# Eight x0 projection panels spread over the forward-transform and spectral stages of a Hyena and gated-linear-attention kernel

## The reference, cut to what matters

```
z = short_conv(u @ w_in + b_in)            # (1024, 3072), three taps along the tokens
x0, x1, v = split(z, 3);  s = v * x1
g = filter(...)                            # taps, 2048 x 1024, divided by their absolute sums
y = irfft(rfft(s, 2048) * rfft(g, 2048))[:1024]
out = ((y + s * skip) * x0) @ w_out + b_out
```

## Time and profile before

| | |
|---|---|
| median of three runs | 2641.41 us |
| the profiled execution | 2642.06 us |
| its span on the core | 2640.3 us |
| TensorE busy | 2469.5 us (94%) |
| GpSimd, VectorE, ScalarE busy | 705.7, 1168.0, 653.2 us |
| mean granted TensorE clock | 0.97 |

### The profile page before, as it was taken

The page is one execution under the profiler, slowest core; times in us unless marked ns, Lnnn a source line. Parts: engine busy times, 40 slices in busy tenths (PEclk is TensorE's granted clock), DMA queues, the critical chain, the costliest instruction groups (busy, mean ns, idle before and its releaser), DMA issues.

```text
span 2640.3 us, 29602 instructions
## 1 busy us (share of the span) xinstructions
PE 2469.5 (94%) x11356; PEld 1979.7 (75%) x11356; DVE 1168.0 (44%) x1221; ACT 653.2 (25%) x800; POOL 705.7 (27%) x394
## 2 busy tenths in 40 slices
PE   7987997677999999999999789999999999999996
PEld 5765664443788888888888679898888787778885
DVE  7899564342623311331235693626262322430443
ACT  4102344344321100000012362626363101111011
POOL 2233112231233333333333312222212232233331
PEclk9998998898999999999999899999999999999998
DMA  4232216776111111111111120202021421211231
GB/s 190 74 126 87 81 63 218 154 172 141 32 43 46 49 51 51 48 48 48 64 48 56 48 96 25 72 24 71 27 69 48 185 91 59 64 40 60 91 120 71
DMA packets 61180, 208.11 MB, mean 79 GB/s; under 512 B 6198, under 2 KB 7928, under 8 KB 60986
## 3 DMA queue, kind: packets, MB, share of 16 engines
q1 hardware_dynamic: 46170, 161.05, 19.2%
q10 hardware_dynamic: 14944, 46.14, 5.9%
HBM read 162.08 MB, written 36.70 MB: 75 GB/s over the span
## 4 chain that ended last, share of the span: by engine, by line
PE 70%; DVE 3%; ACT 1%; issue 0%; ACTq 0%; DVEq 0%
PE ps L1071 59%; PE ps L476 4%; DVE T L1707 1%; PE ps L1315 1%; PE ps L523 1%; PE ps L542 1%; PE ps L505 1%; PE ps L544 1%; PE ps L543 1%; PE ps L1093 0%; DVE XN L1737 0%; PE ps L1102 0%; PE ps L447 0%; DVE X L2017 0%; DVE H L1730 0%; DVE T L1737 0%
## 5 line engine op out<-in xcount | busy, mean ns | idle before, releaser
L1071 PE MATMUL ps<-H,whi 128*128 128x512 f32 x4000 | 1088.3, 394 | 35.2 <-POOL wlo L1027 14.9
L1071 PEld LDWEIGHTS ps<-H,whi 128*128 128x128 f32 x4000 | 753.0, 189 | 208.2 <-issue 23.7
L1025 POOL CAST whi<-wraw 128x1024 fp32r<-128x1024 f32 x190 | 202.9, 1068 | 1808.7 <-issue 744.9
L1071 PE MATMUL ps<-H,wlo 128*128 128x512 f32 x2000 | 618.8, 391 | 0.0
L1027 POOL TENSOR_TENSOR wlo<-wraw,whi 128x1024 fp32r<-128x1024 f32 x194 | 490.8, 2530 | 58.3 <-ACT whi L610 43.1
L1071 PEld LDWEIGHTS ps<-H,wlo 128*128 128x128 f32 x2000 | 377.3, 189 | 79.6
L1071 PE MATMUL ps<-A,whi 128*128 128x512 f32 x1472 | 395.7, 391 | 6.4 <-DVE A L2049 4.9
L1071 PEld LDWEIGHTS ps<-A,whi 128*128 128x128 f32 x1472 | 277.0, 188 | 65.3 <-issue 5.3
L1071 PE MATMUL ps<-A,wlo 128*128 128x512 f32 x736 | 227.2, 390 | 0.0
L1071 PEld LDWEIGHTS ps<-A,wlo 128*128 128x128 f32 x736 | 138.7, 188 | 29.0
L1966 DVE TENSOR_TENSOR T<-ps,T 128x1024 f32<-128x1024 f32 x22 | 26.9, 1224 | 202.6 <-PE ps L1071 202.6
(11 more groups left out here) (342 smaller groups left out, 2587.9 us busy)
## 6 DMA issues: line engine op xcount, KB each, us to landing
wraw<-in_panels SPq DMA_DIRECT2D x181, 512.0 KB, 3.5
mw<-in_modp SPq DMA_DIRECT2D x24, 512.0 KB, 3.5
g<-gsp ACTq DMA_DIRECT2D x16, 512.0 KB, 2.6
wraw<-g SPq DMA_DIRECT2D x16, 512.0 KB, 10.9
s<-sa SPq DMA_DIRECT2D x16, 512.0 KB, 2.6
bs<-s SPq DMA_DIRECT2D x16, 512.0 KB, 6.9
YB<-yi ACTq DMA_DIRECT2D x32, 256.0 KB
kf<-in_kfft SPq DMA_DIRECT2D x16, 320.0 KB, 7.6
```

The costliest lines, as they stand in the source:

```text
L1025: nc.gpsimd.tensor_copy(whi[:, s, :, :], wraw[:, s, :, :]).then_inc(hi_made, 1)
L1071: last = mm(p[:, c * step:(c + 1) * step], w[:, ws, k, :], operand(act, a, k, c * step, step), start=(q == 0 and w is whi and a == 0), sto ...
```

## The change

1. **taps** replaces mix. It has the 16 tap rows alone, unrolled. TensorE makes values two rows ahead and then spreads (`tap_values(m+2)`, `tap_spread(m)`). ScalarE makes the absolute values (into ca or cb) and takes out odd rows, VectorE takes out even rows, SyncE stores both.
2. **sfwd** follows a list. It has four x0 panels among the pairs, and the tap norm moves to its front. `sn`, `st`, `sa` lie elsewhere, so that H stays whole, and there are four `sa` buffers.
3. **spec** has the other four panels, behind groups 1, 4, 7 and 10, in the PSUM tensor `ps[3]`. The spectral work has six banks: four for filter spectra, made one half ahead, one for the signal's spectrum and one for the inverse. VectorE multiplies in place into ga and gb, and `bl`, `kl` are made ahead of the products in its order. The result goes by whole rows to DRAM (`y1`, three `yi` buffers). SyncE reads it back in two halves of 2 MB for partitions 0 to 63 behind groups 13 and 14, and at the end in four pieces of 1 MB for partitions 64 to 127.
4. **inv** has 16 jobs of 256 columns, a piece of 256 channels after the other, with the tiles between.

The lists that set the order of inv, of sfwd and of the late panels:

```diff
-INV = [("rows", 0, 512, n2) for n2 in range(0, N2, 2)]
+INV = [("rows", 0, 256, 4 * _m) for _m in range(4)]
...
+SFWD = [("panel", 0), ("norm",), ("turn", 0), ("turn", 1)]
+for _i in range(PAIRS):
+    SFWD += [("dft", _i, 0), ("dft", _i, 1)]
+    if _i in (2, 5, 7):
+        SFWD.append(("panel", (2, 5, 7).index(_i) + 1))
+    if _i + 2 < PAIRS:
+        SFWD.append(("turn", _i + 2))
+X0_AFTER = (1, 4, 7, 10)
```

SyncE at the end of spec, with `EARLY` = 8:

```diff
+            def y_back(lo, hi, c0, w, k):
+                sp.dma_start(YB[lo:hi, :, c0:c0 + w], y1[lo:hi, :, c0:c0 + w]).then_inc(x_in[k], 16)
...
+                    y_back(0, 8 * EARLY, 512 * (g - 13), 512, g - 13)
+            for n in range(2 * GROUPS - 3, 2 * GROUPS):
+                sp.wait_ge(y1_out[n % 3], y1_stored(n))
+            for k in range(4):
+                y_back(8 * EARLY, P, 256 * k, 256, k)
```

TensorE, spec:

```diff
-                if n >= 2:
-                    pe.wait_ge(spec_ev, n - 1)
+                if n:
+                    pe.wait_ge(spec_ev, n)
...
             filter_spectra(0)
-            filter_spectra(1)
             for n in range(2 * GROUPS):
                 g, c = n // 2, n % 2
-                if n >= 2:
-                    filter_spectra(n)
+                if c and g in X0_AFTER:
...
+                    panel_mm(ps[3], e % 2, H, T, 8).then_inc(panel_done, 1)
+                if n + 1 < 2 * GROUPS:
+                    filter_spectra(n + 1)
                 pe.wait_ge(spec_lo, rows_made(n))
-
-                three(bank(c, 0), g, 0, bh[c][:, :], bl[c][:, :]).then_inc(spec_xm, 1)
+                if n:
+                    pe.wait_ge(spec_y, 2 * n)
+
+                three(bank(4), g, 0, bh[c][:, :], bl[c][:, :], None if c else panel_done).then_inc(spec_xm, 1)
                 if n:
                     inverse(n - 1)
```

ScalarE, taps:

```diff
+            for m in range(N2):
+                if m + 2 < N2:
+                    decay_rows(m + 2)
+                tap_abs(m)
+                if m % 2:
+                    o = spread_job(m)
+                    act.wait_ge(aux_done, A0["taps"] + o + 1)
...
+                    A_(gsp[1][:, :], ps[slot("taps", o)][:, :], ACT.Copy).then_inc(evac[slot("taps", o)], 1)
+                if m + 2 < N2:
+                    decays(m + 2)
```

ScalarE, spec:

```diff
+                if n:
+                    spec_inverse(n - 1)
+                if n + 1 < 2 * GROUPS:
+                    spectra_out(n + 1)
```

VectorE, spec:

```diff
             for n in range(2 * GROUPS):
-                c = n % 2
-                dve.wait_ge(spec_xm, n + 1)
...
+                g, c = n // 2, n % 2
                 if n + 1 < 2 * GROUPS:
                     rows_lo(n + 1)
-                if c == 0 and n // 2 + 1 < GROUPS:
-                    mats_lo(n // 2 + 1)
+                if c == 0 and g + 1 < GROUPS:
+                    mats_lo(g + 1)
...
+                dve.wait_ge(spec_xm, n + 1)
+                for q, t in enumerate((ga, gb)):
+                    dve.wait_ge(spec_g, 2 * n + q + 1)
+                    V_.tensor_tensor(t[c][:, :], ps[2][:, 0:512], t[c][:, :], ALU.mult).then_inc(spec_y, 1)
```

More of the change, by code:

```diff
@@ L959, in _ @@
             panels(N0["up2"] + 2, N0["lrx"])
[L960 removed]
+            sp.wait_ge(aux_done, A0["taps"] + 2 * N2)
             sp.dma_start(wup_h[:, :], d["wup"][:, 0:DK]).then_inc(wup_in, 16)
@@ new lines, in tap_values, with tap_spread @@
+            def tap_values(m):
+                o = tap_job(m)
+                free("taps", o)
+                pe.wait_ge(hbs_made, m + 1)
+                for c in range(2):
+                    last = mm(ps[slot("taps", o)][:, c * 512:(c + 1) * 512], hbs[m % 2][:, :],
+                              wtap[:, c * 512:(c + 1) * 512], start=True, stop=True)
+                last.then_inc(aux_done, 1)
+            def tap_spread(m):
+                o = spread_job(m)
+                free("taps", o)
+                pe.wait_ge(evac[slot("taps", tap_job(m))], turn("taps", tap_job(m)) + 1)
+                for c in range(2):
+                    last = mm(ps[slot("taps", o)][:, c * 512:(c + 1) * 512], cc("dft_g"),
+                              tap[m % 2][:, c * 512:(c + 1) * 512], start=True, stop=True)
+                last.then_inc(aux_done, 1)
@@ L1183, in forward @@
                             last.then_inc(aux_done, 1)
-            pe.wait_ge(const_in, 32)
-            turned(0)
-            for i in range(PAIRS):
-                if i + 1 < PAIRS:
-                    turned(i + 1)
-                forward(i)
-            free("tapnorm", 0)
-            pe.wait_ge(tap_sum, N2)
-            for e in range(KT):
-                last = mm(ps[slot("tapnorm", 0)][:, e:e + 1], gacc[:, e * P:(e + 1) * P], ones[:, 0:1],
-                          start=True, stop=True)
@@ L1196, in _, with tap_norm @@
-            last.then_inc(aux_done, 1)
-            for u in range(3 * PAIRS - 3, 3 * PAIRS):
+            def tap_norm():
+                o = sfwd_job("norm")
+                free("sfwd", o)
+                pe.wait_ge(tap_sum, N2)
+                for e in range(KT):
+                    last = mm(ps[slot("sfwd", o)][:, e:e + 1], gacc[:, e * P:(e + 1) * P], ones[:, 0:1],
+                              start=True, stop=True)
+                last.then_inc(aux_done, 1)
+            pe.wait_ge(const_in, 32)
@@ new lines, in _ @@
+            for kind, *j in SFWD:
+                if kind == "panel":
+                    n = N0["sfwd"] + j[0]
+                    o = sfwd_job("panel", j[0])
+                    pe.wait_ge(split_made, n + 1)
+                    free("sfwd", o)
+                    panel_mm(ps[slot("sfwd", o)], n % 2, H, T, 8).then_inc(panel_done, 1)
+                elif kind == "norm":
+                    tap_norm()
+                elif kind == "turn":
+                    turned(j[0])
+                elif j[1] == 0:
+                    forward(j[0])
@@ new lines, in _, with x0_conv @@
+            for m in range(N2):
+                tap_made(m)
+                if m and m % 2:
+                    o = spread_job(m - 1)
+                    dve.wait_ge(aux_done, A0["taps"] + o + 1)
+                    if m > 2:
+                        dve.wait_ge(g1_out[0], 16 * (m // 2))
+                    V_.tensor_copy(gsp[0][:, :], ps[slot("taps", o)][:, :]).then_inc(evac[slot("taps", o)], 1)
+                tap_added(m)
+            def x0_conv(f):
+                conv(f + 16, f, ca[:, :], G0[:, f, :])
```

428 lines of the change are left out of this document (235 added, 193 removed).

## The result

The changed kernel takes 2670.3 us (median of four runs, 2667.83 to 2672.52), against 2640.52 of the kernel before in the same comparison (four runs, 2635.97 to 2655.18): a ratio of 1.0101, interval 1.0066 to 1.0135. It is slower, by 27 us by the ratio and by 30 by the medians. Its profiled execution has a span of 2670.7 us, 30.4 above the 2640.3 of before.

What follows compares the result with a forecast made beforehand. TensorE was busy 2469.5 us of the span, less in these stages, where stores to 8 partitions paced spec's groups. Terms +40, −2, −20, +2, −2 gave +18.3 on 2642.06: 2660 us, likeliest case 2645 to 2678, whole range 2625 to 2692.

Steps and rivals of the forecast that it cites:

- Taps: Tap rows alone, paced by ScalarE's order, no panel to hide it: 117 us against 76.6 without panels before, +40.
- the clock, 6.4 us: In taps, gaps of about 2 us may drop TensorE's clock: between 5 and 9.5 us lost, 6.4 taken.
- sfwd: Stage with four panels, waits of 6.3 and 5.0 us behind the first two: 90.1 us, 46.3 without panels, −2.
- spec: Stage without ScalarE's 78.7 us wait for stores: 208.8 us, 165.0 without panels against 184.9 before, −20.
- the collision: In spec, VectorE's kl is held behind GpSimd's subtraction: a group without a panel costs 10.2 in place of 7.6 us.
- The clock's 7.5 us: In spec, gaps of 2.5 us cost TensorE clock, 0.75 us each: 7.5 us.
- the read-back's term: In spec, the early read-back of 4 MB delays the loads of groups 13 to 15 by about 3 us.
- Wait ahead of inv: Behind the last inverse, store and first 1 MB piece to 64 partitions: 10.3 us, before 8.7, +2.
- inv: Sixteen jobs +1.5; wait of 1.3 ahead of wout and about 2 of slow start go: 39.7 us, −2.
- C: Slower rival: TensorE's clock falls in every gap of taps and spec, +33 us, 2693 us; chance 0.28.
- A: Rival: GpSimd and VectorE do not meet in spec, 33 us less, 2627 us; chance 0.15.
- D: Rival: quicker handing over, a tap row takes TensorE's own 3.44 us, taps 35 shorter, 2625 us; chance 0.04.

Runs made afterwards that it cites:

- e5b: Changed kernel with two filler matmuls of 512 columns on TensorE ahead of each tap row's values, from row 2 on: 2665.2 us, ratio 1.0101.
- e1: Changed kernel with ScalarE's hbs copies of tap row m+3 ahead of the exponential of row m+2, not behind it: 2650.4 us, ratio 1.0031.
- e7: e1, and VectorE adds row m-1's absolute taps to the sum behind row m's product, not ahead of it: 2628.2 us, ratio 0.9957.
- e4: Changed kernel with the convolutions of x0 panels 0 to 2 behind the reciprocal and next pair's copies in VectorE's order: 2657.3 us, ratio 1.0052.
- e2: Changed kernel with GpSimd's next split released by the odd half's signal matmuls, except in groups a panel follows: 2651.2 us, ratio 1.0035.
- e6: Changed kernel with kl of the next group behind the even half's products in VectorE's order, not ahead of them: 2670.3 us, ratio 1.0107.
- e8: e2, and the early read-back in four 1 MB pieces behind groups 12 to 15, not two of 2 MB: 2639.9 us, ratio 0.9993.
- e11: e10, and seven filler matmuls of 512 columns in TensorE's wait ahead of inv: 2581.4 us, ratio 0.9788.
- e10: e9, and partitions 64 to 95 of the first quarter of columns read back behind group 15: 2582.6 us, ratio 0.9772.
- e9: The changed kernel with the edits of e7, e8 and e4 together: 2584.2 us, ratio 0.9790 to the kernel before.

## Why the prediction was right or wrong, step by step

The forecast was 2660, measured 2670.3: within the stated range, 2.3 us beyond the 2668 from which the prediction counts "slower by over 1%" (0.35); with a ratio of 1.0101, interval 1.0066 to 1.0135, the runs do not tell on which side of 1% it lies. The waits that were named came, but the one in inv that was to go stayed. Four of the five stages were forecast too short, 12.9 us over all, and inside the stages some misses cancel.

* **Taps, +40 forecast, +45.1 measured.** The chain of exponential, hbs, values and spread was right: at full clock a pair costs 11.79 (e5b), worked out 11.64. The term that was too small is the clock, 6.4 us. It was spread over the stage by mean clocks of other stages; in the trace five of six idle times of 2.74 us put the next values at half clock, so a pair is mostly 13.61. By e5b the gaps cost 10.7 us. Two smaller misses nearly cancel: the first spread ended at 254.5, not at 256.3, and from there on the rows take 84.0 us in e5b, where 81.9 were worked out without the clock. Not foreseen, for the order of ScalarE hid it, was VectorE's sum (e1, e7).
* **sfwd, −2 forecast, −0.4 measured.** Both waits came as worked out (6.3 and 5.0; 6.21 and 5.16), the stage 1.6 us over. The first panel takes 12.5 us, the third 11.0: it starts at half clock, behind a wait of 3.91 us in the last tap row. e4 confirms the convolution as cause.
* **spec, −20 forecast, −16.3 measured.** ScalarE's waits for stores went and the collision came; e2, e6 and group 12 confirm it. That four groups take 10.14 to 10.18 us, forecast 10.17, is in part luck. The path was another: TensorE waits for `kl` itself, ahead of the filter spectra, and not for the products behind it (e6). And a group without the collision takes 8.0 us, not the 7.6 worked out, so the collision is worth 2.2 and not 2.6. The clock's 7.5 us, 0.75 in each of ten groups, came otherwise: groups 2, 5 and 8 are 1.9 us longer than 10.17, 1.6 of it TensorE's own work at half clock (9.45 for 7.88), group 0 is 1.4 longer, and the others up to group 12 are not. Too small was the read-back's term, 3 us for late loads: e8 shows 9.0 us of it in a kernel without the collision, 7.0 of them in the waits of groups 14 and 15. I had priced 4 MB as a delay of some loads, not as 20 us in which the kf loads, 320 KB each, stand behind 2 MB pieces at 205 GB/s (in the changed kernel such a load lands 3.1 us after its issue in the median, and 15.7 at the worst).
* **Wait ahead of inv, 10.3 forecast, 10.2 measured.** The half rate taken for 64 partitions, 5 us for the piece, is what flowed. For the stores of before, the prediction calls 61 GB/s measured and 54 worked out an agreement; they are an eighth apart, the measured rate the higher.
* **inv, −2 forecast, +1.3 measured.** The wait at the end did not go: two last tiles stand behind the last job as before, and TensorE waits 1.22 us for ScalarE in all variants; in this trace they then run at half clock (3.42, in most variants 2.20). And the wait of 10 us made the start slow (13.31 for six jobs, 10.57 in e11), where I had let the slow start go.
* **The rivals.** C, the clock falling in every gap, was the nearest: it happened behind five of the six longer idle times of the taps and behind the waits of 2.63 us in spec, but hardly behind the shorter ones, and cost 10.7 us in the taps, not 27. A, no collision, is refuted by the trace; e2 shows its worth, 19 us in spec as it stands and 28 with the loads in time (e8), where I had 33. D, a row at TensorE's own 3.44, is what e7 reaches at 3.7, by another order; as long as ScalarE's order stood, it could not come.

## What to carry to other kernels

When a filler is taken out from between short dependent steps, the orders of all engines must be read anew: an operation that waits (an exponential that waits for its buffer) must not stand ahead of one that could go (the copies for the next row), and the same on the engine that answers it. Here three such places, the release of a split at a moment when its partner engine has nothing of the kind to do, and a read-back in smaller pieces made a change of +30 us into one of −56. Price a gap on TensorE by the matmuls that may follow it at half clock, with a range, for the same gap did and did not bring it; and a large read-back by what queues behind it.

## What the runs showed of the hardware

* In the changed kernel an idle time of 2.74 us ahead of four matmul instructions was followed by half clock (3.40 us for 1.96) in five cases of six; one of 1.83 was not in six of seven (the seventh, the first, came while the clock was still low). In spec 2.63 us were followed by half clock (groups 2, 5, 8) and 2.30 us were not (groups 3, 6, 9, 11).
* The length of the idle time alone does not decide. In e1, of four idle times of 2.64 to 2.81 us ahead of values, two were followed by full clock (four instructions in 1.98) and two were not (2.59 and 3.58). In e4 a pair ran at half clock behind 1.89 us. Ahead of inv's last tiles the same 1.22 us were followed by half clock in four traces of twelve and by full clock in eight.
* VectorE's subtraction `kl`, with two operands in SBUF, is held by GpSimd's subtraction (2.70 us for 0.55), and its products, with one operand in PSUM, are not (0.68), side by side in e6.
* A read of DRAM into the upper 64 partitions flows at 205 GB/s, into all 128 at 423. That 32 of the upper 64 get the same 205 is worked out from e10's wait (2.5 us less for 0.5 MB less); its rate was not measured by itself, for the next pieces were issued right behind it.
* A gain of 2.5 us ahead of a stage can be lost in it: in e10 the six jobs and the last tiles met a slower clock than in e9, and in e11, with matmuls of no use in the wait, inv was 1.6 to 4.0 us shorter than in all the others. Why e10's start was slower than e9's after a shorter wait is not explained; single traces differ by as much without an edit.
